# A hybrid decoder step: the tile rebuilt around channel-wise projections, with rotary embedding and the first sum of the inversion on GpSimd

## Chip, cores, metric

The kernel runs on one NeuronCore of a Trainium2 chip. The metric is device time in microseconds (us), lower is better. TensorE multiplies matrices, VectorE and ScalarE work elementwise and read its results from PSUM, GpSimd works elementwise on SBUF alone, SyncE (SP) starts the transfers.

## The reference

Two layers of a decoder trunk run over a prompt of 2048 tokens and over one new token of 8 sequences. All is fp32. A layer is

```python
h = rmsnorm(x, norm_pre) * (1 + scale) + shift        # shift, scale, gate from c
proj = h @ w_in                                        # 1024 -> 2880 columns
qa, ka, va, ga, pb, gb, xc, gc = split(proj)
q, k = rope(qa), rope(ka)                              # A: 8 query heads, 2 key heads of 64
ya = sink_attention(band of 128 keys back) * silu(ga)
yb = rwkv7_time_mix(pb, gb)                            # B: 4 heads of 64, delta rule, silu gate
yc = rglru_mix(xc, gc)                                 # C: convolution of width 4, gated recurrence of width 256
x = x + gate * rmsnorm(concat(ya, yb, yc) @ w_out, norm_post)
```

B's recurrence per head and token is `s = s*w + (s @ -kk) (kk*a) + v k`, read by `r`. Inputs to it are a token shift `xs = p + (prev - p) * mu`, decays from a low-rank projection of `xs`, and a normalised `kk`.

## The kernel before

All weights of a layer stay in SBUF (`Win`, `Wout`). The prompt is cut into 16 tiles of 128 tokens; after them a layer does the 8 sampled tokens. Every engine runs its own program; semaphores (`s[...]`) join them, and each engine works strictly in the order in which its program is written. The loop over tiles is `Fori(0, NT - 1)` with the last tile written out. `tile(n, ahead)` finishes tile n and, with `ahead`, starts tile n+1 in its last third.

`hT` holds the normalised rows of a tile, transposed (8 slices of 128 channels). The projection by `fill` has a slice of `hT` stationary and up to 512 columns of `Win` moving, so results are token-wise: 128 tokens by columns. What B and C want by channel is copied to SBUF by ScalarE and transposed back by TensorE: `channels_rk` (4 blocks), `channels_vw` (3), the convolution input `xcT_mm` (2) and the gates of B and C `gbcT_mm` (4).

TensorE's order in a tile is: transposes of v and the low-rank products (`vbT_mm`, `lora_mm`, `kksum_mm`); projections of q, of the convolution input and values (`xv_mm`), of the gates of B and C (`gbc_mm`), with the bonus product inside; Gram products of B in blocks of 64 tokens (`gA_mm`, `gB_mm`, `gC_mm`); five levels of the inversion of a unit triangular matrix by squaring (`squares(level)` and `multiply(level)`), with pieces of the attention gate `C_GA`, the RG-LRU gates (`lru_mm`), transposes of q and k, and the first attention scores in between; second scores; the state chain of two blocks (`right_side`, `solve`, `next_state`, `outputs`) with the transposes of probabilities and the products with values between; then projections `fill_rk` and `fill_vwk` of the next tile, transposes of the outputs, and the output projection in two halves (`project`, L757).

x of the next tile is squared by ScalarE (`x_square`), rooted, normalised by VectorE into `xn`, transposed in two halves (`x_lo` into PSUM bank G0, `x_hi` into M3), and scaled into `hT` by ScalarE (`h_lo`) and VectorE (`h_hi`). VectorE also does the token shift, the operands of the Gram products, the rotation of q and k (L1277 to L1282), the masks, half of the inversion's copies and sums, the convolution, scans, row maxima and the normalisations. The inversion starts with

```python
for r in half:
    last = tt(Q[r, :, :], NW[r, 0], over(ident[r, r], 1, U), ALU.add)
```

on VectorE (L1296). Square roots are ScalarE's, each with a load of its table. SyncE's queue holds for each tile: x of the next tile (after `xn_ready`), the table of rotation (after `rope_ready` of the tile before), x again for the residual (after `y_mm`), and the store (after `o_ready`). GpSimd has no program.

Of the kernel before, what the change touches and what calls it, by code (L numbers as in the profile page):

```python
# [46 lines left out]
LNX_EPS = 64e-5  # L47
LRU_C = 8.0
# [59 lines left out]
def over(ap, axis, count):  # L108
# [7 lines left out]
TILE_SEMS = """x_squared rms_root xn_ready xT_lo xT_hi hT_lo hT_hi  # L116
 rk_mm vwk_mm rk_out vwk_out rkT_mm vwT_mm pB_ready q_mm q_out xs_ready carried tw_ready lora_mm vbT_mm vst_ready
 sq_ready kksum_mm sgw_ready a_ready kknorm cum_ready exps_ready bonus_in bd_ready bonus_mm bonus_out
 gA_mm gB_mm gC_mm ntn_ready g_ready gC_ready btT_mm bt_out
 xv_mm xv_out xcT_mm xcb_ready conv_ready lru_mm gates_ready lru_exps lru_t lru_root h_ready yC_ready  # L120
 gbc_mm gbc_out gbcT_mm gates_T ga_mm ga_out
 rope_ready qT_mm kT_mm qT_ready kT_ready qbd
 s0_mm s1_mm neg0 neg1 es0 es1 exp0 exp1 pT0_mm pT1_mm pT0_act pT0_dve pT1_act pT1_dve pv_mm yA_tm yAT_mm yA_ready window_moved
 u_out y_mm y_sq y_root yn_ready ynT_mm yB_ready ytm_ready
 s_mm o0_mm o1_mm o_squared o_root o_ready""".split()
TILE_STEPS = {"inv_mm": 5, "inv_act": 5, "inv_dve": 5, "q_mm5": 5, "q_dve": 4, "rh_ready": 2, "rh_mm": 2, "u_mm": 2,
# [3 lines left out]
ACT_SEMS = """rms_root hT_lo x_squared rk_out vwk_out pB_ready q_out xv_out tw_ready sgw_ready a_ready xcb_ready kknorm  # L130
 exps_ready gbc_out inv_act bt_out gates_T gates_ready lru_exps qT_ready kT_ready lru_root ga_out es0 es1 exp0 exp1
 u_act pT0_act pT1_act y_sq y_root yA_ready o_squared o_root""".split()
PE_SEMS = [k for k in TILE_SEMS + list(TILE_STEPS) if k.endswith("_mm") or k in ("xT_lo", "xT_hi", "q_mm5")]
DVE_SEMS = [k for k in TILE_SEMS + list(TILE_STEPS) if k not in PE_SEMS and k not in ACT_SEMS]
# [28 lines left out]
DVE_X = 5  # L163
DVE_T, DVE_L, DVE_D, YVAR, OVAR, QINIT = 37, 14, 50, 28, 35, 11


def program(nc, d):
    with ExitStack() as ctx:
# [3 lines left out]
        def sem(name):  # L172
# [21 lines left out]
        hT = sb("hT", [P, KC, P])  # L194
# [18 lines left out]
        nstrict = sb("nstrict", [P, 2, CH])  # L213
        Vst = sb("Vst", [P, U, HD])
        G = sb("G", [P, 3, 512])
# [4 lines left out]
        bonv = sb("bonv", [P, 256])  # L220
        xcb = sb("xcb", [P, 2, P + 3])
# [18 lines left out]
        xn = RA[:, 0:1024]  # L240
        ob = RA[:, 1024:2048]
        lu, lgr, lgi, lth, laa, la2, lh = (RA[:, 256 * k:256 * k + 256].rearrange("p (c t) -> p c t", c=2)
                                           for k in range(7))
# [10 lines left out]
            "dve_t", "dve_x", "act_t", "dve_l", "act_l", "zeros", "layer_end", "dve_d")}  # L254
# [64 lines left out]
        rowbuf = [hT[:, 4 * b:4 * b + 4, :].rearrange("p k t -> p (k t)") for b in range(2)]  # L319
# [9 lines left out]
        def _(sp):  # L329
# [7 lines left out]
            for l in range(DEPTH):  # L337
# [27 lines left out]
                with sp.Fori(0, NT - 1) as i:  # L365
                    n = l * NT + i

                    sp.wait_ge(s["xn_ready"], DONE(n))
                    load(i + 1, n + 1)
                    residual_and_store(i, n)  # L370
# [38 lines left out]
        def _(pe):  # L409
# [7 lines left out]
            def fill(out, col, width, ks):  # L417
                for k in ks:
                    last = mm(out[:, 0:width], hT[:, k, :], Win[:, k, col:col + width], start=k == 0, stop=k == KC - 1)  # L419
                return last  # L420
# [7 lines left out]
            with pe.Fori(0, DEPTH) as l:  # L428
# [33 lines left out]
                def x_lo(m):  # L462

                    pe.wait_ge(s["xn_ready"], DONE(m))
                    pe.wait_ge(s["gbc_out"], BEFORE(m))
                    for k in range(4):
                        last = T(G0[:, P * k:P * k + P], xn[:, P * k:P * k + P])
# [8 lines left out]
                def fill_rk(m):  # L476

                    pe.wait_ge(s["hT_lo"], DONE(m))
                    pe.wait_ge(s["hT_hi"], DONE(m))
                    fill(G0, C_R, 512, range(KC)).then_inc(s["rk_mm"], 1)  # L480

                def fill_vwk(m):

                    pe.wait_ge(s["yA_tm"], BEFORE(m))
                    fill(G1, C_V, 448, range(KC)).then_inc(s["vwk_mm"], 1)

                def channels_rk(m):

                    pe.wait_ge(s["rk_out"], DONE(m))
                    pe.wait_ge(s["ytm_ready"], BEFORE(m))  # L490
                    for k in range(4):
                        last = T(M2[:, P * k:P * k + P], stA[:, P * k:P * k + P])
                    last.then_inc(s["rkT_mm"], 1)

                def channels_vw(m):
                    pe.wait_ge(s["vwk_out"], DONE(m))
                    pe.wait_ge(s["yB_ready"], BEFORE(m))
                    T(M3[:, 0:P], stB[:, 0:P])
                    T(M3[:, P:2 * P], stB[:, P:2 * P])
                    T(M3[0:64, 2 * P:3 * P], stB[:, 256:320]).then_inc(s["vwT_mm"], 1)  # L500

                def tile(n, ahead):

                    pe.wait_ge(s["xs_ready"], DONE(n))
                    pe.wait_ge(s["pT1_dve"], BEFORE(n))
# [3 lines left out]
                    pe.wait_ge(s["tw_ready"], DONE(n))  # L509
                    pe.wait_ge(s["pT1_act"], BEFORE(n))  # L510
# [3 lines left out]

                    pe.wait_ge(s["sq_ready"], DONE(n))
# [1225 lines left out]
```

## Time and profile before

| | |
|---|---|
| time, median of 3 runs | 3261.7 us (3260.98 to 3263.45) |
| profiled execution | 3271.33 us |
| its span | 3269.5 us |
| TensorE matmul, busy | 3017.4 us (92%) |
| VectorE, ScalarE, GpSimd, busy | 1750.7, 1429.8, 0.2 us |
| mean granted clock of TensorE | 0.961 |

The span is the profiler's, from the first to the last instruction. Shares are means over setup, 32 tiles and the two sampled steps. In the rows PE is TensorE's matmul, PEld its weight load, DVE VectorE, ACT ScalarE, POOL GpSimd; Lnnn is a line of the kernel. A matmul of fp32 stands there as two instructions, each with its load.

### The profile page before, as it was taken

What the parts mean: (1) busy time and instruction counts of PE and PEld (TensorE: products, weight loads), DVE (VectorE), ACT (ScalarE), POOL (GpSimd) and SP (SyncE); (2) the same over time, 40 slices, a digit from 0 to 9 for tenths busy, and PEclk for the clock granted to TensorE, in tenths of its full rate; (3) what the DMA queues carried; (4) which work ended last, traced back from release to release, by engine and by line L of the source; (5) the groups of instructions that cost most, each with busy time, mean ns of one, the idle gap of its engine ahead of it and who ended that gap; (6) DMA issues with size and microseconds to landing.
All of it is one profiled execution on the core that took longest, in us unless ns stands there. A gap on an engine that the chain in (4) does not pass through costs nothing.

```text
span 3269.5 us, 62255 instructions
## 1 busy us (share of the span) xinstructions
PE 3017.4 (92%) x24404; PEld 1852.7 (57%) x24404; DVE 1750.7 (54%) x4385; ACT 1429.8 (44%) x3055; POOL 0.2 (0%) x4
## 2 busy tenths in 40 slices
PE   4899999999999999998649999999999999999986
PEld 3555556666655555665335555566666655555654
DVE  1455555556555555555414555555566555555554
ACT  0444445445544444544204444454455544445432
POOL 0000000000000000000000000000000000000000
PEclk7999999999999999999769999999999999999996
DMA  9000000000000000000370000000000000000001
GB/s 371 8 20 20 20 20 19 7 20 20 20 13 20 20 20 20 19 7 14 119 289 2 20 20 20 20 19 7 20 20 20 13 20 20 20 20 19 12 9 39
DMA packets 36847, 116.07 MB, mean 36 GB/s; under 512 B 13104, under 2 KB 16304, under 8 KB 36016
## 3 DMA queue, kind: packets, MB, share of 16 engines
q1 hardware_dynamic: 29136, 89.20, 7.8%
q10 hardware_dynamic: 7648, 26.04, 2.1%
q8 instruction: 38, 0.62, 0.1%
q14 instruction: 25, 0.20, 0.0%
HBM read 96.83 MB, written 18.41 MB: 35 GB/s over the span
## 4 chain that ended last, share of the span: by engine, by line
PE 75%; DVE 15%; issue 6%; DMA 2%; ACT 1%; ACTq 0%; DVEq 0%; SPq 0%
PE G L419 37%; PE M L757 14%; PE M L415 5%; PE G L652 4%; DVE small L1367 2%; DMA RB<-in_w_mod 2%; PE M L579 2%; PE M L566 2%; PE G L425 2%; DVE W L1291 1%; DVE RA L1332 1%; DVE Q L1315 1%; PE M L602 1%; PE M L512 1%; PE M L545 1%
## 5 line engine op out<-in xcount | busy, mean ns | idle before, releaser
L419 PE MATMUL G<-w_in,hT 128*128 128x512 f32 (+2 forms) x3072 | 1296.6, 572 | 3.1 <-DVE hT L1212 3.1
L419 PEld LDWEIGHTS G<-w_in,hT 128*128 128x128 f32 x3072 | 571.4, 191 | 552.8 <-issue 474.9
L757 PE MATMUL M<-w_out,yT 128*128 128x512 f32 x1024 | 454.1, 597 | 5.2 <-DVE yT L1446 5.2
L757 PEld LDWEIGHTS M<-w_out,yT 128*128 128x128 f32 x1024 | 191.3, 192 | 223.9 <-issue 223.9
L1224 DVE TENSOR_TENSOR xs<-pB 128x768 f32<-128x768 f32 x32 | 30.7, 959 | 395.8 <-ACT pB L938 395.8
L1315 DVE TENSOR_TENSOR Q<-Q,M 64x256 f32<-64x256 f32 x320 | 133.8, 418 | 119.4 <-PE M L579 115.3
L566 PE MATMUL M<-W 64*64 64x64 f32 x4608 | 163.5, 218 | 7.8 <-DVE W L1291 7.8
L566 PEld LDWEIGHTS M<-W 64*64 64x64 f32 x4608 | 149.4, 135 | 11.3 <-issue 11.3
L630 PE MATMUL M<-kT,stA 64*128 64x256 f32 x512 | 144.3, 402 | 0.0
L652 PE MATMUL G<-Vt,RB 128*128 128x64 f32 x1024 | 127.9, 278 | 0.0
L579 PEld LDWEIGHTS M<-Q,W 64*64 64x64 f32 x2560 | 88.2, 134 | 68.2 <-issue 68.2
L652 PEld LDWEIGHTS G<-Vt,RB 128*128 128x128 f32 x1024 | 119.1, 191 | 4.3
L1035 ACT ACTIVATE RA<-M,small 128x256 f32<-128x256 f32 x256 | 117.3, 472 | 0.0
L984 ACT ACTIVATE W<-M 64x512 f32<-64x512 f32 (+1 forms) x160 | 87.6, 547 | 66.6 <-PE M L566 66.6
L1070 ACT ACTIVATE RB<-M 128x512 f32<-128x512 f32 x32 | 19.1, 598 | 210.3 <-PE M L757 210.3
L972 ACT ACTIVATE xcb<-M 128x256 f32<-128x256 f32 x32 | 12.4, 386 | 222.8 <-PE M L415 222.8
L579 PE MATMUL M<-Q,W 64*64 64x64 f32 x2560 | 107.5, 223 | 2.5
L630 PEld LDWEIGHTS M<-kT,stA 64*128 64x128 f32 x512 | 85.6, 186 | 36.4 <-issue 29.0
L1309 DVE COPY W<-M 64x512 f32<-64x512 f32 (+1 forms) x160 | 102.0, 638 | 6.3
L1291 DVE TENSOR_TENSOR W<-M,nstrict 64x512 f32<-64x512 f32 x64 | 44.1, 689 | 111.1 <-PE M L545 110.6
L415 PE MATMUL M<-cst,RA 128*128 128x128 f32 x642 | 87.8, 284 | 6.4 <-DVE stA L1579 6.4
L927 ACT ACTIVATE stB<-G 128x320 f32<-128x320 f32 x32 | 14.0, 438 | 171.8 <-PE G L419 171.8
(403 smaller groups left out, 4559.2 us busy)
## 6 DMA issues: line engine op xcount, KB each, us to landing
w_in<-in_w_in SPq DMA_DIRECT2D x2, 11520.0 KB, 33.3
xa<-in_x_prompt SPq DMA_DIRECT2D x16, 512.0 KB, 3.6
RA<-in_w_mod ACTq DMA_DIRECT2D x16, 512.0 KB, 6.3
W<-in_w_mod ACTq DMA_DIRECT2D x16, 512.0 KB, 6.5
w_out<-in_w_out SPq DMA_DIRECT2D x2, 4096.0 KB, 36.7
G<-in_x_prompt SPq DMA_DIRECT2D x16, 512.0 KB, 3.3
x_mid<-RA SPq DMA_DIRECT2D x16, 512.0 KB, 2.8
xa<-x_mid SPq DMA_DIRECT2D x16, 512.0 KB, 3.7
```

The lines of the kernel that those rows point to most:

```text
L415: return nc.tensor.transpose(out, in_, ident[0:rows, 0:rows])
L419: last = mm(out[:, 0:width], hT[:, k, :], Win[:, k, col:col + width], start=k == 0, stop=k == KC - 1)
L566: last = mm(m[r, 256 * w + CH * u:256 * w + CH * u + CH], NW[r, 1 - w, u, :], NW[r, w, u, :], start=True, stop=True)
L579: last = mm(m[r, 256 + CH * u:256 + CH * u + CH], NW[r, 1, u, :], Q[r, u, :], start=True, stop=True)
L630: last = mm(m[:, 256 * c:256 * c + 256], qT[HD * g:HD * g + HD, 2 * j + c, :], kT[HD * g:HD * g + HD, :], start=False, stop=True, skip_gro ...
L652: last = mm(G1[:, HD * (4 * j + k):HD * (4 * j + k) + HD], PT[:, f, k, :], Vt[:, f, HD * g:HD * g + HD], start=f == 0, stop=f == 1)
L757: last = mm(o[:, :], yT[:, k, :], Wout[:, k, 512 * h:512 * h + 512], start=k == 0, stop=k == KC - 1)
L984: A(NW[half[0], w:], M0[half[0], 256 * w:512].rearrange("p (w u c) -> p w u c", u=U, c=CH), ACT.Copy).then_inc(s["inv_act"], 1)
L1035: last = A(Pm[:, j, k, :], m[:, 256 * (k // 2):256 * (k // 2) + 256], ACT.Exp, bias=small[:, 16 + 4 * j + k:17 + 4 * j + k], scale=SCALE, ...
L1291: last = tt(NW[r], m[r, :].rearrange("p (w u c) -> p w u c", w=2, c=CH), over(nstrict[r], 2, U), ALU.mult)
L1309: cp(NW[half[1], w:], M1[half[1], 256 * w:512].rearrange("p (w u c) -> p w u c", u=U, c=CH))\
L1315: last = tt(Q[r, :, :], Q[r, :, :], m[r, 256:512].rearrange("p (u c) -> p u c", c=CH), ALU.add)
```

## The change

- The projections of r, k, v, the low ranks, the convolution input and the gates of B and C have the weights stationary and 128 tokens moving (`channels`), and give channels at once; the transposes back go. q, the keys, the values and the attention gate stay token-wise.
- `hT` has two buffers, and the loop takes two tiles. The gates of B and C (`gates(j)`) are projected late, into G0, between the steps of the state chain, after the second half of x's transposes, which now also goes to G0.
- The convolution input comes first in a tile, then q; the RG-LRU gates come before the last quarter of q. The low-rank products and the normalising sums (`front`) and the operands (`operands`) of the next tile move up between the halves of the output projection.
- GpSimd does the rotation (five instructions on 128 partitions, 320 or 640 elements in each), the first sum of the inversion, and the roots of x, y and the output as powers of -0.5. VectorE squares and sums y. SiLU of the attention gate is taken later from a plain copy; SiLU of the gates of B and C goes straight from PSUM to `yT`.

```diff
-            def fill(out, col, width, ks):
+            def fill(out, H, col, width, ks):
                 for k in ks:
-                    last = mm(out[:, 0:width], hT[:, k, :], Win[:, k, col:col + width], ...)
+                    last = mm(out[:, 0:width], H[:, k, :], Win[:, k, col:col + width], ...)
+            def channels(out, H, col, width):
+                for k in range(KC):
+                    last = mm(out[0:width, :], Win[:, k, col:col + width], H[:, k, :], start=k == 0, stop=k == KC - 1)
...
                 def x_hi(m):
-                    pe.wait_ge(s["pT0_act"], BEFORE(m))
+                    pe.wait_ge(s["hT_lo"], DONE(m))
                     for k in range(4, 8):
-                        last = T(M3[:, P * (k - 4):P * (k - 4) + P], xn[:, P * k:P * k + P])
+                        last = T(G0[:, P * (k - 4):P * (k - 4) + P], xa[:, P * k:P * k + P])
...
+                def fill_rk(m, H):
+                    pe.wait_ge(s["hT_hi"], DONE(m))
+                    pe.wait_ge(s["gbc_out"], BEFORE(m))
+                    for j in range(4):
+                        last = channels(G0[:, P * j:P * j + P], H, C_R + P * j, P)
+                def fill_vwk(m, H):
+                    for j in range(2):
+                        channels(G1[:, P * j:P * j + P], H, C_V + P * j, P)
+                    channels(G1[:, 2 * P:3 * P], H, C_WA, 64)
+                    fill(G1[:, 3 * P:4 * P], H, C_KA, P, range(KC))
...
+                def tile(n, b, ahead):
+                    pe.wait_ge(s["vwk_out"], DONE(n))
+                    for j in range(2):
+                        channels(G1[:, P * j:P * j + P], H, C_XC + P * j, P)
+                    fill(G1[:, 2 * P:3 * P], H, C_VA, P, range(KC)).then_inc(s["xv_mm"], 1)
+                    fill(G0, H, C_Q, 512, range(0, 6))
+                    pe.wait_ge(s["conv_ready"], DONE(n))
+                    for k in range(4):
+                        last = mm(M3[:, P * k:P * k + P], gatew[:, k, :], lu[:, k % 2, :], start=True, stop=True)
+                    fill(G0, H, C_Q, 512, range(6, KC)).then_inc(s["q_mm"], 1)
...
                     pe.wait_ge(s["gC_ready"], DONE(n))
+                    pe.wait_ge(s["q_init"], DONE(n))
                     multiply(1)
...
                     scores(0, M3, M4).then_inc(s["s0_mm"], 1)
                     multiply(5)
+                    if ahead:
+                        x_lo(n + 1)
...
+                    def gates(j):
+                        return channels(G0[:, P * j:P * j + P], H, C_GB + P * j, P)
...
                     scores(1, M0, M1).then_inc(s["s1_mm"], 1)
+                    if ahead:
+                        x_hi(n + 1)
                     right_side(0)
+                    if ahead:
+                        pe.wait_ge(s["hT_hi"], DONE(n + 1))
+                    gates(0)
                     solve(0)
                     probs(0, M3, M4).then_inc(s["pT0_mm"], 1)
                     next_state(0)
                     outputs(0).then_inc(s["s_mm"], 1)
-                    if ahead:
-                        x_lo(n + 1)
+                    gates(1)
...
                     outputs(1).then_inc(s["y_mm"], 1)
+                    gates(2)
+                    gates(3).then_inc(s["gbc_mm"], 1)
                     values(1).then_inc(s["pv_mm"], 1)
...
         @block.scalar
                     exps(0, M3, M4, s["neg0"], s["es0"], s["exp0"])
+                    if ahead:
+                        h_lo(n + 1, hT[:, 1 - b])
+                    solved(0)
...
+        @block.gpsimd
+                def x_root(m):
+                    pool.wait_ge(s["x_squared"], DONE(m))
+                    xlink(ts(small[:, 1:2], small[:, 0:1], D * EPS, None, ALU.add))
+                    tt(small[:, 7:8], small[:, 1:2], minus, ALU.pow).then_inc(s["x_root"], 1)
+                def tile(n, ahead):
+                    pool.wait_ge(s["q_out"], DONE(n))
+                    tt(r4[:, :, 0, :], q4[:, :, 1, :], over(rope[:, 32:64], 1, 10), ALU.mult)
+                    link(tt(r4[:, :, 1, :], q4[:, :, 0, :], over(rope[:, 32:64], 1, 10), ALU.mult))
+                    link(tt(qk..., qk..., over(rope[:, 0:32], 1, 20), ALU.mult))
+                    tt(q4[:, :, 0, :], q4[:, :, 0, :], r4[:, :, 0, :], ALU.subtract)
+                    tt(q4[:, :, 1, :], q4[:, :, 1, :], r4[:, :, 1, :], ALU.add).then_inc(s["rope_ready"], 1)
+                    pool.wait_ge(s["ntn_ready"], DONE(n))
+                    tt(Q[:, :, :], NW[:, 0], over(eye[:, :], 1, U), ALU.add).then_inc(s["q_init"], 1)
+                    if ahead:
+                        x_root(n + 1)
+                    pool.wait_ge(s["y_sums"], DONE(n))
...
+                    pool.wait_ge(s["o_squared"], DONE(n))
...
         @block.vector
                     def power_T(level):
                         dve.wait_ge(s["inv_mm"], STEP(n, level, 5))
+                        if level == 1:
+                            dve.wait_ge(s["q_init"], DONE(n))
```

## Rows read from the trace of the kernel before

**Rows 1.** the page: the span, and part 1, busy time of each engine

```profile
span 3269.5 us, 62255 instructions
...
PE 3017.4 (92%) x24404; PEld 1852.7 (57%) x24404; DVE 1750.7 (54%) x4385; ACT 1429.8 (44%) x3055; POOL 0.2 (0%) x4
```

**Rows 2.** windows, one tile from projection to projection: PE, PEld, DVE, ACT, POOL busy, clock, DMA

```profile
820.14:910.61 90.47, 88.07 (x717) 53.92 (x717) 51.93 (x128) 43.37 (x95) 0.00 (x0) 1.00 0.05 18
```

**Rows 3.** the chain that ended last: start us, us, what

```profile
820.14 6.87 PE M L757 x16
```

**Rows 4.** timeline of TensorE's weight loads, same tile: start us, us, what, xcount

```profile
864.85 0.97 PEld L602 LDWEIGHTS M<-RA,gatew 128*128 128x128 f32 x8 [1.11 <-DVE xcb L1335]
...
889.05 1.86 PEld L652 LDWEIGHTS G<-Vt,RB 128*128 128x128 f32 x16
```

**Rows 5.** timeline of TensorE's matmuls, same tile; in brackets idle time before

```profile
819.54 0.60 PE L415 MATMUL M<-cst,stA 128*128 128x128 f32 x4
819.98 7.03 PE L757 MATMUL M<-w_out,yT 128*128 128x512 f32 x16
...
855.61 0.68 PE L545 MATMUL M<-kr,bk 64*64 64x64 f32 x16
...
858.34 1.15 PE L566 MATMUL M<-W 64*64 64x64 f32 x32 [0.24 <-DVE W L1291]
...
862.32 0.63 PE L579 MATMUL M<-Q,W 64*64 64x64 f32 x16
...
864.85 1.16 PE L602 MATMUL M<-RA,gatew 128*128 128x128 f32 x8 [0.97 <-DVE xcb L1335]
...
879.54 0.68 PE L579 MATMUL M<-Q,W 64*64 64x64 f32 x16
...
883.18 0.33 PE L662 MATMUL M<-S,kr 64*64 64x64 f32 x4 [0.20 <-DVE Q L1315]
...
884.64 0.45 PE L673 MATMUL M<-RH,Q 64*64 64x64 f32 x8 [0.78 <-DVE RH L1380]
...
887.37 0.28 PE L703 MATMUL M<-Vst,G 64*64 64x64 f32 x4
887.79 0.66 PE L415 MATMUL G<-cst,RA 128*128 128x128 f32 x4
```

**Rows 6.** timeline of VectorE, same tile

```profile
848.04 0.49 DVE L1277 TENSOR_TENSOR RB<-qk,rope 128x320 f32<-128x320 f32 x1
...
850.24 0.48 DVE L1282 TENSOR_TENSOR qk<-qk,RB 128x320 f32<-128x320 f32 x1
...
860.43 0.69 DVE L1309 COPY W<-M 64x512 f32<-64x512 f32 x1
861.15 0.86 DVE L1321 TENSOR_TENSOR G<-M,cst 64x256 f32<-64x256 f32 x2
862.04 0.60 DVE L1328 TENSOR_SCALAR RA<-xcb,prm 128x128 f32<-128x128 f32 x2
...
864.62 0.17 DVE L1335 COPY xcb<-xcb 128x6 f32<-128x6 f32 x1
...
880.52 1.29 DVE L1367 TENSOR_REDUCE small<-M 128x2 f32<-128x512 f32 x2
...
882.12 0.15 DVE L1372 TENSOR_TENSOR small<-prm,small 128x4 f32<-128x4 f32 x1
...
893.21 1.37 DVE L1212 TENSOR_SCALAR hT<-M,gs,mod 128x128 f32<-128x128 f32 x4
```

**Rows 7.** timeline of ScalarE, same tile

```profile
843.04 0.60 ACT L964 ACTIVATE qk<-G 128x512 f32<-128x512 f32 x1
...
884.12 0.21 ACT L1035 ACTIVATION_READ_ACCUMULATOR RA<-M,small 128x1 f32 x1
...
888.54 1.52 ACT L913 ACTIVATE hT<-G,mod,gs 128x128 f32<-128x128 f32 x4
```

**Rows 8.** groups of VectorE by line: xcount, busy us, mean ns of one, idle before

```profile
L1254 DVE RECIPROCAL W<-W 128x256 f32<-128x256 f32 x32 | 56.1, 1753 | 1.1
```

More of the change, by code:

```diff
@@ L113, in over @@
     return v.to_broadcast(shape)
[L116 to L122, printed above, removed]
+TILE_SEMS = """x_squared x_root xn_ready xT_lo xT_hi hT_lo hT_hi
+ rk_mm vwk_mm rk_out vwk_out pB_ready q_mm q_out xs_ready carried tw_ready lora_mm vbT_mm vst_ready
+ sq_ready kksum_mm sgw_ready a_ready cum_ready exps_ready bonus_in bd_ready bonus_mm bonus_out
+ gA_mm gB_mm gC_mm ntn_ready q_init g_ready gC_ready btT_mm bt_out
+ xv_mm xv_out conv_ready lru_mm gates_ready lru_exps lru_t lru_root yC_ready kknorm
+ gbc_mm gbc_out ga_mm ga_copied ga_out
+ rope_ready qT_mm qT_ready kT_ready
@@ L133 @@
 PE_SEMS = [k for k in TILE_SEMS + list(TILE_STEPS) if k.endswith("_mm") or k in ("xT_lo", "xT_hi", "q_mm5")]
-DVE_SEMS = [k for k in TILE_SEMS + list(TILE_STEPS) if k not in PE_SEMS and k not in ACT_SEMS]
+POOL_SEMS = "rope_ready q_init x_root y_root o_root".split()
+DVE_SEMS = [k for k in TILE_SEMS + list(TILE_STEPS) if k not in PE_SEMS + ACT_SEMS + POOL_SEMS]
 PE_STEPS = """ssq_mm proj_mm perm_mm lora_mm kk_mm lru_mm bonus_mm sa_mm vb_mm sr_mm s_mm mean_mm var_mm pt_mm pv_mm o_mm
@@ L625, in scores @@
+                    multiply(4)
+                    squares(5)
                     def scores(j, ma, mb):
-                        for g, m in ((0, ma), (1, mb)):
+                        for m in (ma, mb):
                             mm(m[:, :].rearrange("p (c k) -> p c k", c=2), identb[:, :], over(mk[:, :], 1, 2),
                                start=True, stop=False, skip_group_check=True)
-                            for c in range(2):
+                        for c in range(2):
+                            for g, m in ((0, ma), (1, mb)):
@@ L632, in scores @@
                         return last
-                    multiply(4)
-                    squares(5)
                     pe.wait_ge(s["qT_ready"], DONE(n))
@@ L671, in solve @@
                             u = NCH * p + m
-                            for r, b in zip(half, HB):
-                                last = mm(b[r, HD * p:HD * p + HD], Q[r, u, :], RH[r, p, :], start=True, stop=True)
+                            for r, o in zip(half, HB):
+                                last = mm(o[r, HD * p:HD * p + HD], Q[r, u, :], RH[r, p, :], start=True, stop=True)
                         last.then_inc(s["u_mm"], 1)
@@ L1281, in tile @@
-                    tt(q4[:, :, 0, :], q4[:, :, 0, :], r4[:, :, 0, :], ALU.subtract)
-                    tt(q4[:, :, 1, :], q4[:, :, 1, :], r4[:, :, 1, :], ALU.add).then_inc(s["rope_ready"], 1)
-                    dve.wait_ge(s["bonus_mm"], DONE(n))
-                    tt(bonv[:, :], G1[:, 0:256], xsv, ALU.mult).then_inc(s["bonus_out"], 1)
-                    dve.wait_ge(s["gA_mm"], DONE(n))
-                    o = CST["mst"][0]
-                    later = cst[:, o:o + 512]
-                    for r, m in zip(half, (M0, M1)):
-                        last = tt(NW[r], m[r, :].rearrange("p (w u c) -> p w u c", w=2, c=CH), over(nstrict[r], 2, U),
-                                  ALU.mult)
@@ L1318, in tile @@
-                    power_T(1)
-                    dve.wait_ge(s["gC_mm"], DONE(n))
-                    for r, m in zip(half, HB):
-                        last = tt(G3T[r], m[r, 0:256].rearrange("p (u c) -> p u c", c=CH), over(con("mit")[r, r], 1, U),
-                                  ALU.mult)
-                    last.then_inc(s["gC_ready"], 1)
-                    dve.wait_ge(s["xcb_ready"], DONE(n))
+                    dve.wait_ge(s["xv_out"], DONE(n))
                     cw, cb = par("cw"), par("cb")
@@ L1461, in tile @@
                     link.end()
-                for step in (x_mean, x_norm, h_hi, token_shift):
-                    step(l * NT)
-                with dve.Fori(0, NT - 1) as i:
-                    tile(l * NT + i, True)
-                tile(l * NT + NT - 1, False)
+                x_mean(l * NT)
+                h_hi(l * NT, hT[:, 0])
+                token_shift(l * NT)
+                operands(l * NT)
+                with dve.Fori(0, NT // 2 - 1) as i:
+                    tile(l * NT + 2 * i, 0, True)
+                    tile(l * NT + 2 * i + 1, 1, True)
+                tile(l * NT + NT - 2, 0, True)
+                tile(l * NT + NT - 1, 1, False)
                 dve.wait_ge(s["o_ready"], BEFORE((l + 1) * NT))
```

542 lines of the change are left out of this document (258 added, 284 removed).

## The prediction

> **What bounds the kernel now.** I read the page's table of busy time first: TensorE is busy for 92% of the span, VectorE for 54%, ScalarE for 44%, and GpSimd does nothing [rows 1]. The window of one steady tile, from one output projection to the next, is sharper: 88.07 of 90.47 us are TensorE's, at the full granted clock [rows 2]. The chain that ended last is made of TensorE's groups; one of them, 16 instructions of 512 columns, takes 6.87 us, 0.429 us each or 0.84 ns a column [rows 3]. So a tile's time is the length of TensorE's program plus the gaps in it. The timeline of TensorE has four gaps worth a name: 0.24 us before the first squaring, 0.97 us before the RG-LRU gates (the convolution is late), 0.20 us before the right side, 0.78 us before the first solve [rows 5]. That is 2.19 us of the tile. Less work on VectorE or ScalarE is worth nothing by itself; only what shortens TensorE's program or these gaps is worth something, and any new gap costs its whole length.
>
> **Projections turned to channels.** An fp32 matmul is two instructions of each kind, so 512 columns over 8 slices of K were 16 pairs. With the weights of the projection stationary and 128 tokens moving, 128 columns of output cost 16 pairs of weight load and 128-column matmul: 64 pairs for r and k; 64 for v, the low ranks and the keys; 48 for the convolution input and the values; 64 for the gates of B and C. Only q and the attention gate keep the 512-column form. A 128-column matmul at 0.84 ns a column is 0.107 us, but each now needs its own load. Two rows show the pace of loads: one load lasts 0.19 us and overlaps the next; 8 of the RG-LRU gate weights take 0.97 us, so (0.97 - 0.19)/7 = 0.111 us apart, and 16 of the value products take 1.86, so 1.67/15 = 0.111 us [rows 4]. I take 0.111 us a pair (0.107 for the 16 of the 64 low-rank channels, whose loads are narrower). The four groups then cost 7.12, 7.05, 5.34 and 7.12 us where 512, 448, 384 and 512 columns cost 6.87, 6.01, 5.15 and 6.87: **+1.73 us** a tile. The bounds are 0.107 (columns alone, +0.8 us) and 0.121, what the 8 loads take with the start of their group in the count (0.97/8, +4.1 us).
>
> **Transposes gone.** Four of r and k, three of v and the low ranks, two of the convolution input and four of the gates go, 13 in all, at 0.44 us for four [rows 5]: **-1.43 us**. The copies and transposes of these on ScalarE and the smaller moves to other lines lie on engines that are half idle.
>
> **Gaps that close.** The convolution now starts at the copy of the first projection of the tile (5.34 us in, 0.8 us for signal and copy), and TensorE has 12 instructions of q (5.15 us) ahead of the RG-LRU gates. VectorE needs 2.75 us for it (862.04 to 864.79 [rows 6]), and must be through with the operands, the residual and the copies of v first; laid out with the durations of before, about 1.7, 4.4 and 5.7 us into the tile. So the convolution ends at 8.9 us, and TensorE asks at 10.5: the 0.97 is gone, with 1.6 us to spare. The gaps of 0.20 and 0.78 go too, since x's second half, a gate projection and their waits stand there now, and so do 0.3 us that the first x transposes waited for the normalised rows (887.79, where the products before it stand 0.12 us apart [rows 5]): **-2.25 us**. The 0.24 stays.
>
> **Two waits that come.** (1) The second half of x's transposes is written into the same bank as the first (G0), so TensorE waits there for `hT_lo`. ScalarE makes that after the first exponentials, which wait for the maxima. From the end of the first scores: 0.2 us to VectorE, 1.75 us of maxima (880.52 to 882.27), 2.06 us of exponentials (to 884.33), 1.52 us for four scalings, 0.1 us back: 5.6 us [rows 6, 7]. TensorE has the last product and the second scores (879.54 to 882.98, 3.44 us [rows 5]) and four transposes (0.43) until then, 3.87 us. It stands for **1.76 us**, with everything behind it in its queue. Before, ScalarE did these scalings after both sets of exponentials, with TensorE busy. (2) The gates of B and C are projected into G0 too, so the first waits for `hT_hi`: 0.2 + 1.37 + 0.1 us after the transposes [rows 6], of which the right side (0.68 us) covers some: **0.99 us**. The right side's negation comes 0.6 us later on VectorE and is hidden by the gate projection. Together **+2.75 us** in each of the 30 tiles that prepare a next one. The last tile of a layer has neither.
>
> So far +1.73 - 1.43 - 2.25 + 2.75 = **+0.8 us** a tile, which is within what a reading of 0.1 us steps can give.
>
> **GpSimd in the inversion's path.** This is the term that I am least sure of. Rotary embedding starts when q is copied; the first sum of the inversion (`q_init`) comes behind it in GpSimd's queue, and both halves of the first power's copy and `multiply(1)` wait for `q_init`. Count from the tile's start on TensorE: 5.34 (convolution input, values) + 6.87 (q) + 1.0 (RG-LRU gates, as their loads) + 0.43 (the bonus product, 512 columns) = 13.64 us, when the Gram products begin. q is complete at 13.2, and with 0.2 us of signal and 0.60 us of copy [rows 7] GpSimd starts at 14.1. In the trace 6.71 us lie between the Gram products and the first product (855.61 to 862.32 [rows 5]), so TensorE asks for it at 20.35. Between `q_init` and TensorE stand VectorE's copy of the power (0.69), the masking of the third Gram matrix (0.86 [rows 6]) and two signals, 1.8 us. GpSimd therefore has 20.35 - 14.1 - 1.8 = 4.45 us. No row shows an elementwise instruction on GpSimd. From below: VectorE does the five of the rotation in 2.68 us (848.04 to 850.72 [rows 6]) and a sum of 256 elements in about 0.43, 3.11 us, and there is no stall. From above: the slowest elementwise instruction of the trace, VectorE's reciprocal, takes 1753 ns for 256 elements [rows 8], 6.85 ns each; 1920 + 256 elements would take 14.9 us, a stall of 10.4. I take twice VectorE, 6.22 us (near the middle of the two ends in ratio, 6.8): a stall of **1.77 us** in each of 32 tiles. TensorE has nothing else to do there, and nothing later makes up for it, since the rest of the tile's order hangs on the levels that follow.
> The Trainium skill, GPSIMD Engine Reference (Performance versus the Vector engine), speaks against this part of the change: elementwise work belongs on VectorE, and a two-input add of 2048 fp32 elements is 1.96 times slower on GpSimd. By that factor the 3.11 us are 6.1, the stall 1.65 us and the whole 3337 us; no run here shows it yet.
>
> **Small roots on GpSimd.** The root of x must be there 1.9 us after the sum of squares, that of y has over 5 us. The root of the output, three instructions, must be there within 2.6 us before the convolution comes too late. At the 0.15 us of VectorE's four-element instruction [rows 6] all are hidden; at 1.75 us each [rows 8] the last would cost 2.7 us a tile and x's 1.6. I take nothing. The transfers stay early: x's rows are asked for some 5 us into a tile, take under 4, and are squared at about 31; the table of rotation waits for `rope_ready` at about 20 in SyncE's queue, and what is queued behind it (the residual) is not wanted before 55. The second hT buffer and the loop over two tiles add no instructions per tile.
>
> **Ends.** In the first tile of a layer the decays and operands have no projection of 6.87 us over them, against a slack of 1.6 us and 4 us of residual work that is not there yet: the convolution is 1.3 us late, twice. Last tiles: 2.75 us less, twice.
>
> **The sum.** 30 x 0.8 = 24; 2 x (0.8 - 2.75) = -3.9; 2 x 1.3 = 2.6; 32 x 1.77 = 56.6: +79 us. The profiled execution took 3271.3 us (a span of 3269.5 and 1.8 around it), 9.6 over the median of the runs. 3271.3 + 79.3 - 9.6 = **3341 us**, 2.4% slower.
>
> **The rivals.**
> (A) GpSimd is quick enough: a rotation and sum within 4.45 us. Then 3341 - 57 = 3284 us. For it: the slack is 1.4 times VectorE's time. Against: nothing in the trace; two operands and chained waits.
> (B) GpSimd is much slower, three times VectorE or more (9.3 us): a stall of 4.9 us, 3341 + 32 x 3.1 = 3440 us; at the upper bound 3619. For it: the patterns are cut into runs of 32 elements, and each step waits for the one before. Small roots that overrun 2.6 us come to the same side.
> (C) Faster: ScalarE's `hT_lo` is not late, and the two waits for G0 don't open. The place is the stretch between the first scores and the right side. With both gone and GpSimd within its slack the time is 3284 - 30 x 2.75 = 3202 us. It decides from the point where the two waits and the stall of GpSimd together are under 1.95 us a tile (2.75 - 0.8). For it: one signal or overlap that I misjudge by 0.5 us at each of three places. Against: the 5.6 us are read from rows almost whole.
> (D) Loads and matmuls of a pair overlap less than I take, 0.121 us a pair throughout: 240 x 0.010 = +2.4 us a tile, 3341 + 77 = 3418 us. Against it: two rows of loads at 0.111.
>
> **How the numbers follow.** The forecast, with stalls of 1 to 3 us, has 0.50; A 0.17; B 0.17; C 0.12; D 0.04. A difference of 0.2% (6.5 us) is about what a measurement of this kernel can tell from none. C holds nearly all of faster (0.12); A spreads to both sides of its 3284 by half a microsecond a tile, so 0.06 is within 0.2%; the rest, 0.82, is slower. The forecast's own range is 3315 to 3380. The range of 8 in 10 reaches over A (3265) and into B (3425).
>
> **What would show it.** A tile of some 93 us between output projections. Weight loads of the projections 0.111 us apart. A gap of about 1.8 us before the second x transposes, released by ScalarE's scaling; one of 1 us before the first gate projection, by VectorE's; one of 1.8 us before `multiply(1)`, led back to GpSimd. No gap before the RG-LRU gates. Wrong would be: no gap at G0 (C), GpSimd's five instructions in under 3.5 us (A) or over 9 (B), or a gap where I see none, as before the RG-LRU gates for want of the output's root.

## The result, and the profile after

| | before | this |
|---|---|---|
| time, median | 3261.34 us (4 runs, 3260.91 to 3263.45) | 3416.01 us (4 runs, 3411.9 to 3429.6) |
| ratio | | 1.048, interval 1.0448 to 1.0512 |
| mean granted clock of TensorE | 0.961 | 0.938 |

The kernel is 155 us slower; the forecast was 79. The page of the changed kernel gives the span, the busy times and the queue that fetches instructions:

```profile
span 3410.2 us, 72041 instructions
...
PE 3060.1 (90%) x29620; PEld 2304.3 (68%) x29620; DVE 1633.0 (48%) x3973; ACT 1194.1 (35%) x2707; POOL 285.8 (8%) x421
...
q8 instruction: 262, 4.29, 0.5%
```

VectorE and ScalarE lost 118 and 236 us of work against [rows 1], and nothing came of it. TensorE is busy 43 us longer, yet 98 us more of the span are not its own. The windows show a tile from projection to projection, as [rows 2], and then single stretches (busy time by engine, granted clock, share of DMA, GB/s):

```profile
857.38:953.14 95.76, 88.86 (x882) 67.43 (x880) 48.32 (x115) 35.85 (x82) 8.94 (x13) 0.98 0.06 19
819.70:822.30 2.60, 2.16 (x20) 1.65 (x20) 1.40 (x5) 0.00 (x0) 0.00 (x0) 0.50 0.00 0
822.30:826.00 3.70, 3.68 (x16) 3.48 (x16) 2.13 (x7) 0.00 (x0) 0.00 (x0) 0.50 0.02 4
911.00:916.10 5.10, 2.06 (x14) 1.18 (x14) 2.31 (x7) 3.43 (x13) 0.00 (x0) 1.00 0.00 0
918.20:921.80 3.60, 3.53 (x17) 3.41 (x17) 2.18 (x8) 0.00 (x0) 0.00 (x0) 0.54 0.02 5
```

The tile is 5.29 us longer, and its clock is no longer 1.00: there is a stretch at 0.50, TensorE's lower level of 1.2 GHz, in it (918.20 to 921.80) and in the tile before (819.70 to 826.00). What TensorE waited for in the whole run (us in all, times, longest), and one wait of VectorE:

```profile
PE G L421 <- ACT hT L905: 95.9, 32, 3.1
PE M L577 <- DVE G L1341: 48.1, 32, 1.7
...
PE G L430 <- DVE hT L1235: 20.6, 32, 1.8
PE M L577 <- issue: 17.1, 32, 0.5
...
PE M L529 <- DVE xcb L1303: 7.3, 12, 0.8
...
DVE Vst L1290 <- issue: 23.2, 12, 2.1
```

The first three are the ones forecast: x's second half (`x_hi`) waits for `hT_lo`, `multiply(1)` for what hangs on GpSimd's sum, the first gate projection for `hT_hi`. The other three were not: `multiply(5)` (L577, released by nothing that the profile names), the RG-LRU gates (L529) in 12 tiles, and a pause of VectorE before L1290 in the same 12. The timeline of TensorE, to be laid beside [rows 5]:

```profile
884.35 1.16 PE L529 MATMUL M<-RA,gatew 128*128 128x128 f32 x8 [0.63 <-DVE xcb L1303]
...
895.96 0.68 PE L577 MATMUL M<-Q,W 64*64 64x64 f32 x16 [1.54 <-DVE G L1341]
...
907.96 0.61 PE L615 MATMUL M<-mk,identb 128*128 128x512 bf16 x2
908.50 1.14 PE L619 MATMUL M<-kT,stA 64*128 64x256 f32 x8
910.17 0.68 PE L577 MATMUL M<-Q,W 64*64 64x64 f32 x16 [0.54 <-issue]
910.90 0.66 PE L421 MATMUL G<-cst,xa 128*128 128x128 f32 x4
911.40 0.59 PE L615 MATMUL M<-mk,identb 128*128 128x512 bf16 x2
911.92 1.13 PE L619 MATMUL M<-kT,stA 64*128 64x256 f32 x8
916.15 0.66 PE L421 MATMUL G<-cst,xa 128*128 128x128 f32 x4 [3.09 <-ACT hT L905]
...
918.27 3.60 PE L430 MATMUL G<-hT,w_in 128*128 128x128 f32 x16 [0.85 <-DVE hT L1235]
...
924.74 2.05 PE L430 MATMUL G<-hT,w_in 128*128 128x128 f32 x16
...
937.62 7.36 PE L430 MATMUL G<-hT,w_in 128*128 128x128 f32 x64
```

The same 16 instructions of a gate projection take 3.60 us behind the wait of 3.09 us and 2.05 us six microseconds later. VectorE around the scores, to be laid beside [rows 6]:

```profile
880.31 1.19 DVE L1290 COPY Vst<-M 64x128 f32<-64x128 f32 x4 [1.96 <-issue]
...
908.56 0.86 DVE L1360 TENSOR_TENSOR_SCAN lh<-RA,hcar 128x128 f32<-128x128 f32 x2
...
909.64 0.43 DVE L1329 COPY W<-M 64x256 f32<-64x256 f32 x1
910.10 0.75 DVE L1230 TENSOR_SCALAR xa<-xa,small 128x1024 f32<-128x1024 f32 x1
910.88 1.29 DVE L1370 TENSOR_REDUCE small<-M 128x2 f32<-128x512 f32 x2
```

ScalarE, the same stretch, beside [rows 7]:

```profile
912.67 0.20 ACT L1001 ACTIVATE small<-small 128x4 f32<-128x4 f32 x1 [2.92 <-DVE small L1375]
...
914.58 1.52 ACT L905 ACTIVATE hT<-G,mod,gs 128x128 f32<-128x128 f32 x4
```

The first scores end on TensorE at 909.63 (`multiply(5)` starts at 910.17, after 0.54 of idle time). VectorE begins the maxima 1.25 us later, since the scans, the power's copy and the normalisation of x stand ahead of them. GpSimd, which no row of before could show:

```profile
874.01 0.47 POOL L1138 TENSOR_TENSOR small<-small 128x1 f32<-128x1 f32 x1 [32.41 <-ACT RB L1043]
...
874.98 0.57 POOL L1141 TENSOR_TENSOR small<-small,expo 128x1 f32<-128x1 f32 x1
888.18 0.86 POOL L1121 TENSOR_TENSOR RB<-qk,rope 128x320 f32<-128x320 f32 x1 [12.63 <-ACT qk L960]
...
889.94 1.54 POOL L1123 TENSOR_TENSOR qk<-qk,rope 128x640 f32<-128x640 f32 x1
...
893.30 0.73 POOL L1130 TENSOR_TENSOR Q<-W,eye 128x256 f32<-128x256 f32 x1
```

Rotation and sum take 888.18 to 894.03, 5.85 us; the root of the output 1.54.

### The profile page after: what moved, and what is told of

It reads as the page before. It is cut to its first block, busy times and chain, and to the rows that moved or that the text cites. A ratio compares the mean times of both kernels' runs of the same rounds, so it can differ in the third digit from the quotient of the medians.

```text
span 3410.2 us, 72041 instructions
## 1 busy us (share of the span) xinstructions
PE 3060.1 (90%) x29620; PEld 2304.3 (68%) x29620; DVE 1633.0 (48%) x3973; ACT 1194.1 (35%) x2707; POOL 285.8 (8%) x421
## 3 DMA queue, kind: packets, MB, share of 16 engines
q8 instruction: 262, 4.29, 0.5%
## 4 chain that ended last, share of the span: by engine, by line
PE 58%; issue 19%; DVE 11%; POOL 6%; ACT 4%; DMA 2%; DVEq 0%; ACTq 0%; POOLq 0%; SPq 0%
PE G L430 17%; PE G L425 12%; PE M L752 7%; PE M L421 3%; PE G L641 3%; PE M L564 3%; PE M L577 2%; PE G L436 2%; DMA RA<-in_w_mod 2%; ACT RA L1004 2%; POOL qk L1123 1%; ACT hT L905 1%; DVE small L1370 1%; DVE hT L1235 1%; PE G L421 1%
## 5 line engine op out<-in xcount | busy, mean ns | idle before, releaser
L430 PE MATMUL G<-hT,w_in 128*128 128x128 f32 (+1 forms) x6656 | 847.3, 289 | 20.6 <-DVE hT L1235 20.6
L430 PEld LDWEIGHTS G<-hT,w_in 128*128 128x128 f32 (+1 forms) x6656 | 815.3, 199 | 49.5 <-DVE hT L1235 22.2
L425 PE MATMUL G<-w_in,hT 128*128 128x512 f32 (+1 forms) x2048 | 608.4, 442 | 0.0
L425 PEld LDWEIGHTS G<-w_in,hT 128*128 128x128 f32 x2048 | 296.4, 191 | 168.0 <-issue 159.3
L577 PEld LDWEIGHTS M<-Q,W 64*64 64x64 f32 x2560 | 89.1, 134 | 134.6 <-issue 134.6
L577 PE MATMUL M<-Q,W 64*64 64x64 f32 x2560 | 109.3, 224 | 65.3 <-DVE G L1341 48.1
L421 PE MATMUL G<-cst,xa 128*128 128x128 f32 x256 | 52.5, 340 | 110.4 <-ACT hT L905 95.9
L1012 ACT ACTIVATE Ub<-M 64x128 f32<-64x128 f32 x128 | 34.8, 272 | 327.8 <-PE M L662 327.1
L421 PEld LDWEIGHTS G<-cst,xa 128*128 128x128 f32 x256 | 33.6, 168 | 127.9 <-ACT hT L905 108.7
L913 ACT ACTIVATE pB<-G 128x512 f32<-128x512 f32 x32 | 19.1, 597 | 276.1 <-PE G L430 276.1
L1442 DVE COPY Ep<-M 64x256 f32<-64x256 f32 x64 | 26.7, 417 | 178.2 <-PE M L421 177.8
```

Of the source, the lines that this page charges most:

```text
L421: return nc.tensor.transpose(out, in_, ident[0:rows, 0:rows])
L425: last = mm(out[:, 0:width], H[:, k, :], Win[:, k, col:col + width], start=k == 0, stop=k == KC - 1)
L430: last = mm(out[0:width, :], Win[:, k, col:col + width], H[:, k, :], start=k == 0, stop=k == KC - 1)
L577: last = mm(m[r, 256 + CH * u:256 + CH * u + CH], NW[r, 1, u, :], Q[r, u, :], start=True, stop=True)
```

## The experiments

Each is timed beside the kernel before on the same chip, and its ratio is against that. Differences between two changed kernels are of medians, partly from different chips, on which the kernel before took 3261 to 3265 us. "This" is the changed kernel, whose +155 us is to be taken apart.

### The order of ScalarE: the first scaling before the exponentials

```diff
+                    if ahead:
+                        h_lo(n + 1, hT[:, 1 - b])
                     exps(0, M3, M4, s["neg0"], s["es0"], s["exp0"])
-                    if ahead:
-                        h_lo(n + 1, hT[:, 1 - b])
```

> ScalarE scales the first half of x (h_lo) ahead of the first exponentials instead of behind them. Theory W (the wait of 3.1 us before the second x transposes is ScalarE's order, and the fall of the granted clock to half in the 4 us behind it is caused by that wait): the wait goes nearly whole and the first gate projection takes 1.9 us instead of 3.6; 30 tiles x (3.0 + 1.7 to 2.3) = 140 to 160 us less than the changed kernel, near 3265. Theory O (the length is set by the chain of VectorE and the state, and the wait only moves to the first gate projection or the first probabilities): under 40 us less. A rival on the clock: it falls at this place whatever the wait, and 90 us go.

Measured: 3263.24 us, ratio 0.999 (0.9973 to 1.0006): 153 us under this, level with before. TensorE's timeline:

```profile
605.90 1.14 PE L619 MATMUL M<-kT,stA 64*128 64x256 f32 x8
607.13 0.66 PE L421 MATMUL G<-cst,xa 128*128 128x128 f32 x4
...
609.25 2.05 PE L430 MATMUL G<-hT,w_in 128*128 128x128 f32 x16 [0.85 <-DVE hT L1235]
```

and its tile in the windows:

```profile
561.00:651.90 90.90, 87.71 (x883) 66.38 (x882) 48.23 (x115) 36.60 (x84) 8.93 (x13) 1.00 0.06 19
```

The wait for `hT_lo` is gone from these tiles (3.2 us are left of 95.9 in the whole run), the clock is 1.00 through the tile, and the first gate projection takes 2.05 us. Its own wait grows from 20.6 to 28.8 us, so the two waits explain 84 of the 153 us. The page of this kernel has TensorE busy for 2989.8 us where it was 3060.1 with as many instructions, 70 less: that is about the rest.

### The wait covered with useless work

Three slices of the attention gate's projection are computed again, into a bank that is free, ahead of `x_hi`. This adds work and leaves ScalarE's order alone.

```diff
                     if ahead:
+                        pe.wait_ge(s["ga_copied"], DONE(n))
+                        for k in range(3):
+                            mm(G1[:, :], H[:, k, :], Win[:, k, C_GA:C_GA + 512], start=True, stop=True)
                         x_hi(n + 1)
```

> The changed kernel with three useless 512-column matmuls (2.57 us, into a bank whose content is no longer wanted) in front of the second x transposes, where TensorE waits 3.1 us. Their results are thrown away. Theory W: the work lies in the wait and the clock no longer falls after it, so the kernel with more work is 50 to 65 us faster than the changed kernel (30 x 1.7 to 2.2), and the first gate projection takes 1.9 us. Rival: the slow gate projection has a cause of its own (loads of weights after a pause, the bank), and the time stays within 10 us.

Measured: 3352.16 us, ratio 1.0263 (1.023 to 1.0295), 64 us under this, though TensorE has 180 matmul instructions more. Timeline and window:

```profile
613.72 1.13 PE L619 MATMUL M<-kT,stA 64*128 64x256 f32 x8
614.78 2.84 PE L704 MATMUL G<-w_in,hT 128*128 128x512 f32 x6
617.93 0.66 PE L421 MATMUL G<-cst,xa 128*128 128x128 f32 x4 [0.31 <-ACT hT L908]
...
620.05 2.05 PE L430 MATMUL G<-hT,w_in 128*128 128x128 f32 x16 [0.85 <-DVE hT L1238]
```
```profile
620.00:622.00 2.00, 1.95 (x16) 1.86 (x16) 1.92 (x5) 0.00 (x0) 0.00 (x0) 1.00 0.00 0
```

The second transposes start 4.21 us after the start of the second scores' last group, and 4.23 us after it in this (916.15 - 911.92). So they come no sooner; only TensorE was busy instead of idle, and the clock stayed at 1.00. The 64 us are the price of the clock alone: 2.1 us in each of 30 tiles. The rival of the expectation, that the gate projection is slow for a cause of its own, is out: it takes 2.05 us here, at the same place.

### GpSimd's sum before its rotation

```diff
+                    pool.wait_ge(s["ntn_ready"], DONE(n))
+                    tt(Q[:, :, :], NW[:, 0], over(eye[:, :], 1, U), ALU.add).then_inc(s["q_init"], 1)
                     pool.wait_ge(s["q_out"], DONE(n))
                     tt(r4[:, :, 0, :], ...)                       # rotation
...
-                    pool.wait_ge(s["rope_ready"], DONE(n))
-                    pool.wait_ge(s["ntn_ready"], DONE(n))
-                    tt(Q[:, :, :], NW[:, 0], over(eye[:, :], 1, U), ALU.add).then_inc(s["q_init"], 1)
```

> GpSimd does the first sum of the inversion before the rotation instead of behind it. Theory W: multiply(1) no longer waits 1.5 us, the rotation comes 0.7 us later and is still early: 32 x 1.5 = 48 us less than the changed kernel. Rival: the sum waits for the masked Gram products, which come 2.0 us after q, so the rotation starts 2.7 us later and the transposes of q wait for it instead: no gain, or under 15 us.

Measured: 3357.32 us, ratio 1.0275 (1.0244 to 1.0306), 59 us under this, 1.83 a tile. The wait of 48.1 us is no longer among TensorE's; that of `x_hi` stays at 95.9. The stall on GpSimd, forecast at 56.6 us, is thereby right in place and near in size. The wait itself is 48.1 us, 1.50 a tile; the other 11 us that came back with it are not assigned.

### The projections token-wise again

`fill` with 512, 448, 384 and 512 columns takes the place of the channel-wise products. The results are not transposed, so this kernel's output is not the reference's; the time is that of the products alone.

```diff
-                    for j in range(4):
-                        last = channels(G0[:, P * j:P * j + P], H, C_R + P * j, P)
-                    last.then_inc(s["rk_mm"], 1)
+                    fill(G0, H, C_R, 512, range(KC)).then_inc(s["rk_mm"], 1)
...
-                        return channels(G0[:, P * j:P * j + P], H, C_GB + P * j, P)
+                        return fill(G0, H, C_GB, 512, range(2 * j, 2 * j + 2))
```

> All projections with 512, 448, 384 and 512 columns moving again, in the places of the channel-wise ones and without their transposes, so that r, k, v, the low ranks, the convolution input and the gates of B and C arrive with tokens and channels exchanged: the output is not the reference's, the time is that of the order of the changed kernel with the cheaper products. By the records of the changed kernel (0.115 us a pair against 0.107): 2.7 us a tile, 85 us less, and up to 50 more where the slow clock covers 128-column pairs. By the price of the forecast (0.111): 1.7 us a tile, 55 us less. If the columns alone set the pace: 0.8 us a tile, 27 us less.

Measured: 3351.03 us, ratio 1.0257 (1.0227 to 1.0287), 65 us under this, 2.03 a tile. `x_hi` still waits 95.7 us, and the mean clock is 0.934, so the lower clock is in this time too.

### The kernel before with the new order of the score products

The diff also changed the order inside `scores`: the products of the two key heads, on the channels 0 to 63 and 64 to 127, alternate. I had taken that for nothing. Here it is alone, in the kernel before:

```diff
-                        for g, m in ((0, ma), (1, mb)):
+                        for m in (ma, mb):
                             mm(m[:, :]..., identb[:, :], over(mk[:, :], 1, 2), ...)
-                            for c in range(2):
+                        for c in range(2):
+                            for g, m in ((0, ma), (1, mb)):
                                 last = mm(m[:, 256 * c:256 * c + 256], qT[HD * g:...], kT[HD * g:...], ...)
```

> The kernel before with one part of the change alone: in the attention scores the matmuls of the two key heads alternate (rows 0 to 63 and 64 to 127 of the array in turn), which in the changed kernel's trace shortens each set of scores from 2.8 to 1.7 us. Theory S (VectorE sets when the right side starts: the maxima start at 880.52 behind the scans, whatever TensorE does): no gain, and a wait of some 2.4 us instead of 0.2 before the right side, which may bring the clock down as in the changed kernel and cost up to 2 us a tile: 0 to 60 us slower. Theory T (TensorE is the bound, its shorter program counts): 32 x 2.2 = 70 us faster.

Measured: 3313.35 us, ratio 1.015 (1.0129 to 1.017), 50 us slower than before, by a change that shortens TensorE's program. TensorE:

```profile
885.60 1.13 PE L631 MATMUL M<-kT,stA 64*128 64x256 f32 x8
889.25 0.33 PE L663 MATMUL M<-S,kr 64*64 64x64 f32 x4 [2.51 <-DVE Q L1316]
...
891.08 1.60 PE L415 MATMUL M<-cst,RA 128*128 128x128 f32 x8
```

VectorE, and windows across the wait and behind it:

```profile
885.17 0.86 DVE L1357 TENSOR_TENSOR_SCAN RA<-RA,hcar 128x128 f32<-128x128 f32 x2
...
886.59 1.29 DVE L1368 TENSOR_REDUCE small<-M 128x2 f32<-128x512 f32 x2
...
888.26 0.84 DVE L1316 TENSOR_TENSOR Q<-Q,M 64x256 f32<-64x256 f32 x2
```
```profile
886.70:889.20 2.50, 0.04 (x2) 0.00 (x0) 2.32 (x7) 2.04 (x5) 0.00 (x0) 1.00 0.00 0
891.50:893.00 1.50, 1.50 (x15) 1.17 (x14) 1.05 (x5) 0.53 (x2) 0.00 (x0) 0.51 0.00 0
```

The two sets of scores are 2.3 us shorter together (1.60 + 1.67 where they took 2.76 + 2.82). But VectorE has scans, maxima and the last sum in a row and is not a moment earlier, so the right side now waits 2.51 us where it waited 0.20 [rows 5], 2.3 us more: what the scores gave, the wait took. In the whole run that wait is 79.6 us, where it was 5.9. The 50 us are what the clock cost on top. It falls behind this wait as well: the eight transposes at L415 take 1.60 us, and 1.09 in the kernel before (at 885.01). Before, the slow score products were cover.

### Both orders, then the scans late

The first kernel has the first and the third edit together:

> Both repairs of order together: ScalarE's scaling of x ahead of the first exponentials, GpSimd's first sum ahead of the rotation. Theory W: the two waits lie one behind the other on TensorE, so the gains add: 3263 - 59 = 3204 us, with 5 more or less, which is below the kernel before. Rival: with the first wait gone VectorE's chain up to the right side sets the time and the second repair only moves the wait: 3240 to 3263 us.

Measured: 3202.43 us, ratio 0.9813 (0.9796 to 0.9831), 61 us under the first edit alone, where the third alone gave 59 to this. The terms add.

The next kernel also moves the RG-LRU scans on VectorE:

```diff
-                    for c in range(2):
-                        last = nc.vector.tensor_tensor_scan(lh[:, c, :], ...)
...
                     rhs(0)
+                    for c in range(2):
+                        last = nc.vector.tensor_tensor_scan(lh[:, c, :], ...)
                     maxima(1, M0, M1, s["s1_mm"], s["neg1"])
```

> e7_both, and VectorE does the two scans of the RG-LRU after the first right side instead of before the last copy of the inversion. In the changed kernel's trace TensorE waits 0.54 us before multiply(5), because that copy comes behind the scans. Theory W: that wait goes: 32 x 0.5 = 17 us less than e7_both. Rival: the 1.0 us moves in front of the second maxima and delays the second exponentials and the state chain: no change or up to 15 us more.

Measured: 3184.32 us, ratio 0.9754 (0.9733 to 0.9774), 18 us less; the wait before `multiply(5)` is gone, which was 17.1. The power's copy (909.64 above) had stood behind the scans, and that was the change's own doing: the kernel before does the copy first.

```profile
877.58 0.43 DVE L1309 COPY W<-M 64x256 f32<-64x256 f32 x1
...
879.10 0.86 DVE L1356 TENSOR_TENSOR_SCAN RA<-RA,hcar 128x128 f32<-128x128 f32 x2
```

### The loop written out

The first edit, with `Fori(0, NT // 2 - 1)` of TensorE, ScalarE and VectorE written out:

```diff
-                with pe.Fori(0, NT // 2 - 1) as i:
+                for i in range(NT // 2 - 1):
```

> The kernel of e1_hlo_first with the seven turns of two tiles written out on TensorE, ScalarE and VectorE, so that no branch is taken between tiles. Theory C: in every second tile VectorE stands 2.0 us without a releaser behind the residual, at the place where its loop branches back, and TensorE then 0.6 us before the RG-LRU gates (12 times, 7.3 us in all in the changed kernel); this is loading of code and goes: 5 to 15 us less than e1_hlo_first. Rival: straight code must be loaded too, more of it, and the time stays or grows by 5 to 30 us.

Measured: 3253.0 us, ratio 0.9955 (0.9937 to 0.9973); 10 us under the first edit, the intervals just touching. VectorE's 12 pauses before L1290 and TensorE's 12 waits before the RG-LRU gates are both gone, which ties them together. A loop of seven turns branches back six times in each of two layers, 12 times.

### Three on top of the late scans

Written out as well, rotation back on VectorE, and token-wise (again with untransposed results, not the reference's output):

> e8_scans_late with the tiles written out as in e5_unrolled. Theory C: VectorE's pause at the branch goes here too: 5 to 12 us less than e8_scans_late (10 in e5 against e1). Rival: the later kernel has other slack before the RG-LRU gates, and nothing changes.

> e8_scans_late with the rotation back on VectorE, behind the copy of the second power (GpSimd keeps the first sum and the roots). VectorE needs 2.7 us for it in a pause of 1.8 us. Theory W: TensorE's waits set the time and VectorE has room: within 10 us of e8_scans_late, so that GpSimd's part in the rotation is worth nothing once the order is right. Rival: VectorE is short of time in the inversion, the 2.7 us or part of them reach multiply(3): 30 to 80 us more.

> e8_scans_late with the token-wise projections of e4_tokenwise, at the full clock this time; r, k, v, the low ranks, the convolution input and the gates arrive untransposed, so the output is not the reference's. It sizes what the narrow products cost: by the changed kernel's records (0.115 us a pair) 2.7 us a tile, 86 us less; by the forecast's 0.111 us 1.7 us a tile, 55 us less; by the columns alone 27 us less. The 65 us of e4 lay between, with the slow clock over part of it. Taken from 3184 us: 3098, 3129 or 3157.

| kernel | us | ratio | against late scans |
|---|---|---|---|
| late scans | 3184.32 | 0.9754 (0.9733 to 0.9774) | |
| written out | 3171.42 | 0.9714 (0.9701 to 0.9727) | -13 |
| rotation on VectorE | 3180.52 | 0.9755 (0.9735 to 0.9774) | none |
| token-wise | 3115.59 | 0.9546 (0.9527 to 0.9565) | -69 |

The written-out kernel is the fastest that gives the reference's output, 93 us (2.9%) faster than the kernel before. The rotation costs nothing on either engine once the sum doesn't stand behind it: the ratios, each taken on its own chip, are the same. The token-wise products put the price of the channel-wise ones at 69/32 = 2.15 us a tile, between the two prices expected (1.7 and 2.7).

## Why the prediction was right or wrong

The kernel is slower, and the three waits that were named are there. The size is twice the forecast: 3416 us lie above its own range of 3315 to 3380 and only inside the range of 8 in 10, which reached to 3425 for the sake of rival B. Term by term, for the tile 857.38 to 953.14:

| term of the sum, us a tile | forecast | measured | from |
|---|---|---|---|
| channel-wise products | +1.73 | +2.15 | token-wise run |
| transposes gone | -1.43 | -1.43 | taken as forecast |
| gaps closed | -2.25 | -1.62 | RG-LRU gates 0.63 late |
| shorter scores | 0 | -2.2 | 2 x (2.76 - 1.67) |
| `x_hi` waits | +1.76 | +3.09 | timeline |
| first gate projection waits | +0.99 | +0.85 | timeline |
| `multiply(1)` waits | +1.77 | +1.54 | timeline |
| `multiply(5)` waits | 0 | +0.54 | timeline |
| clock at its lower level | 0 | +2.1 | covered run |
| sum | +2.57 | +5.02 | tile: 95.76 - 90.47 = +5.29 |

0.3 us of the tile stays unassigned. The run that moved GpSimd's sum gave back 1.83 us a tile, 0.3 more than the wait of 1.54; whether that is the same 0.3 no run shows. The 2.1 of the clock is the mean of 30 tiles; in this one the gate projection alone shows 3.60 - 2.05 = 1.55. That the sum is only 2.5 us a tile off is partly luck: terms that were too low or missing make 5.0, and 2.6 were on the other side, most of it the shorter scores, which the forecast didn't see. 2.76 us are the first scores of before (four groups up to `multiply(5)` at 879.54 in [rows 5]), 1.67 those at 907.96.

**The steps that were mis-sized.** The channel-wise products: the pace of 0.111 us a pair was nearly right (64 instructions in 7.36 us are 0.115 each), and 2.15 lies inside the bounds of 0.8 and 4.1. The wait of `x_hi`: I took 5.6 us of chain against 3.87 of cover; it is 6.52 against 3.43 (909.63 to 916.15, less 3.09), and 0.54 of this cover is the wait before `multiply(5)`. The chain is 0.9 us longer because maxima start 1.25 us after the scores, not 0.2: I took that time for a signal's delay and did not ask what VectorE has ahead in its queue. The trace of before could have told: its maxima start at 880.52 [rows 6], 0.90 us after the first scores' end (878.49 + 1.13), behind the scans. The cover is less because the second scores are shorter too. GpSimd: 5.85 us against 6.22. Its time to spare was worked out 0.1 us too short, since 13.2 + 0.2 + 0.60 is 14.0 and not 14.1. The Trainium skill, GPSIMD Engine Reference (Performance versus the Vector engine), gives a factor of 1.96; here 5.85 / 3.11 = 1.9, and the trace agrees. The roots end within their time, at 0.22 to 0.57 us an instruction.

**The step that was missing.** I held TensorE's clock at the 1.00 of [rows 2], though my own forecast put new idle time of 1.8 us and 1 us into the tile. That a wait of 3.09 us is followed by some microseconds at 0.50 costs 64 us, the largest single term of those that were missed. The covered run shows it apart from everything else: same start of `x_hi`, more work, 64 us less.

**The edits that were overlooked.** The alternating score products take 2.2 us less of TensorE and, in the kernel before, make the whole 50 us slower. The Trainium skill, TensorE: Matmul & The Clock Gate (Part 3, packing small matmuls), says that products on different parts of the array run at the same time; the trace agrees, with 1.14 us for eight instructions (908.50 above) that took 1.13 for each four in the kernel before:

```profile
877.11 1.13 PE L630 MATMUL M<-kT,stA 64*128 64x256 f32 x4
...
878.49 1.13 PE L630 MATMUL M<-kT,stA 64*128 64x256 f32 x4
```

In the changed kernel its share can't be read off alone: it takes 1.1 us of work and some cover ahead of `x_hi`. A run of the changed kernel with the old order was not made. The scans, which the change put ahead of the last power's copy, are the other one: 0.54 us a tile before `multiply(5)`, for which the forecast had nothing.

**The convolution.** I had 1.6 us to spare; 12 of 32 tiles have none, since VectorE pauses for 1.96 us before L1290. The Trainium skill, Runtime: NRT & Kernel Launch (Instruction fetch mechanics), says that a taken branch whose target isn't in the fetched pages stalls for the fetch. The trace agrees in that the pause stands at the loop's turn, 12 times, and goes when the loop is written out. The kernel before, whose loop takes one tile, has no such pause, and its queue that fetches instructions moved 0.62 MB against 4.29 (written out it moves 3.93 and VectorE doesn't pause, so the amount alone makes no pause). That points at a branch back over the doubled body; the doubled body was not tried alone.

**The rivals.** B and D give 3440 and 3418 us, near what was measured, but neither happened: GpSimd is 1.9 times VectorE, not 3, and pairs are 0.115 us apart, not 0.121. C's place, ScalarE between the scores, was the right one to look at: with `hT_lo` made early the kernel is level with before, with the sum ahead of the rotation too 3202 us. That is C's number to the microsecond, but by luck: the gate projection still waits there (28.7 us in all), and the shorter scores are not in C's sum.

## What to carry to other kernels

Where a change opens an idle stretch on TensorE, price what comes after it at the lower clock too; filling the stretch with any matmul on free data tells in one run how much of the loss is the clock. When TensorE's work between two waits gets shorter, ask what the other engine has in its queue there: what the forecast took for a signal of 0.2 us was 1.25 us, and most of that was work. A queue's order is cheap to change: one call moved on ScalarE was worth 153 us, one on GpSimd 60, and the large rebuild around them became 2.9% faster instead of 4.8% slower.

## What the runs showed that was not expected

- Behind a wait of 3.09 us in every tile, or one of 2.51 us in the kernel before with alternating scores, the granted clock stands at about 0.50 for a stretch. It reads 1.00 while TensorE waits (911.00 to 916.10, 886.70 to 889.20) and 0.50 to 0.54 only behind it. In the tile before, which had the same wait, the four transposes right behind it were already slow (1.11 us at 819.75); in the one shown they were not (0.66 at 916.15), and the slow stretch began at the gate projection.
- GpSimd: two-operand instructions on 128 partitions take 0.73 us for 256 elements, 0.86 for 320, 1.54 for 640; a power of one element 0.57.
